# A prefill and decode step of a hybrid attention layer: cached values copied to DRAM before cached keys

## The reference, cut to what matters

```
proj = x @ w_in                                  # (576, 1024) @ (1024, 4096)
q, k, v, g_att, gb, gc, hh, g_conv = split(proj, 8)
o_att = dilated_attention(q, concat(k_past, k), concat(v_past, v))   # windows 128/1, 512/4, 2048/16
att = o_att * silu(g_att)
u = gc * hh;  z = gb * conv3(u) * silu(g_conv)
y = LayerNorm(alpha * x + concat(att, z) @ w_out)
new_k, new_v = the last 2048 rows of concat(k_past, k), concat(v_past, v)
```

## Time and profile before

| | |
|---|---|
| Median of 3 runs | 360.97 us (359.77 to 361.14) |
| The profiled execution | 360.34 us, span 358.5 us |
| Granted clock of TensorE, mean share of full | 0.997 |
| TensorE busy | 348.7 us (97%) |
| VectorE, ScalarE busy | 202.1 us (56%), 117.4 us (33%) |
| DMA moved | 141.06 MB, mean 393 GB/s |
| Of it SyncE's queue q1 | 73.20 MB |
| Of it ScalarE's queue q10 | 67.37 MB |
| Chain that ended last | PE 82%, DMA 6%, DVE 5%, SPq 4%, ACT 1% |

### The profile page before, as it was taken

One profiled execution on the slowest core, in us unless ns is written; L12 is line 12 of the kernel. 1 busy time (PEld: TensorE's weight loads), 2 busy tenths in 40 slices (PEclk: granted clock), 3 DMA queues, 4 the chain that ended last, 5 costly groups with the idle time before them and its releaser, 6 DMA issues.

```text
span 358.5 us, 7719 instructions
## 1 busy us (share of the span) xinstructions
PE 348.7 (97%) x3280; PEld 311.6 (87%) x3280; DVE 202.1 (56%) x381; ACT 117.4 (33%) x233; POOL 11.6 (3%) x28
## 2 busy tenths in 40 slices
PE   8999999999999999999999999999999999899992
PEld 6998888899989888999988889998879988688782
DVE  3724528764145558541446484613546598886774
ACT  4623324352153323421433333214441824330000
POOL 0000000000100000001000000000000004000000
PEclk9999999999999999999999999999999999999998
DMA  8999999999999999999999999999999999999991
GB/s 293 399 429 415 417 415 418 416 423 418 419 421 417 417 413 388 403 420 395 401 416 414 421 419 419 424 423 419 419 414 415 415 402 321 404 345 370 350 324 67
DMA packets 34836, 141.06 MB, mean 393 GB/s; under 512 B 3441, under 2 KB 3825, under 8 KB 32753
## 3 DMA queue, kind: packets, MB, share of 16 engines
q1 hardware_dynamic: 18338, 73.20, 50.8%
q10 hardware_dynamic: 16464, 67.37, 47.6%
HBM read 135.80 MB, written 71.86 MB: 579 GB/s over the span
## 4 chain that ended last, share of the span: by engine, by line
PE 82%; DMA 6%; DVE 5%; SPq 4%; ACT 1%; issue 0%; DVEq 0%; ACTq 0%
PE pj_a L1153 9%; PE pj_b L1153 9%; PE pj_b L1155 8%; PE pj_a L1155 8%; PE pj_a L1154 8%; PE pj_b L1154 8%; DMA wo_raw<-in_w_out 6%; PE sc L1310 4%; PE sc L1346 4%; PE px L1258 3%; PE po L1290 2%; PE pt L1276 2%; SPq L374 2%; SPq L303 2%; PE px L1503 2%; PE px L1504 2%
## 5 line engine op out<-in xcount | busy, mean ns | idle before, releaser
L1153 PE MATMUL pj_b<-x_hi,w_hi 128*128 128x288 f32 x248 | 75.1, 303 | 0.7 <-DVE mix L908 0.7
L1153 PE MATMUL pj_a<-x_hi,w_hi 128*128 128x288 f32 x248 | 75.7, 305 | 0.0
L1154 PE MATMUL pj_a<-x_lo,w_hi 128*128 128x288 f32 x248 | 73.2, 295 | 0.0
L1154 PE MATMUL pj_b<-x_lo,w_hi 128*128 128x288 f32 x248 | 73.1, 295 | 0.0
L1155 PE MATMUL pj_b<-x_hi,w_lo 128*128 128x288 f32 x248 | 73.0, 294 | 0.0
L1155 PE MATMUL pj_a<-x_hi,w_lo 128*128 128x288 f32 x248 | 72.9, 294 | 0.0
L785 DVE TENSOR_TENSOR w_lo<-w_raw,w_hi 128x1024 fp32r<-128x1024 f32 x30 | 36.7, 1223 | 32.3 <-ACT w_hi L472 32.3
L472 ACT CAST w_hi<-w_raw 128x1024 fp32r<-128x1024 f32 x30 | 31.4, 1047 | 69.2 <-DMA w_raw<-in_w_tiles 45.3
L1153 PEld LDWEIGHTS pj_a<-x_hi,w_hi 128*128 128x128 f32 x248 | 46.5, 187 | 6.8 <-issue 6.2
L1153 PEld LDWEIGHTS pj_b<-x_hi,w_hi 128*128 128x128 f32 x248 | 46.5, 187 | 3.1 <-issue 1.1
L1155 PEld LDWEIGHTS pj_b<-x_hi,w_lo 128*128 128x128 f32 x248 | 46.7, 188 | 0.0
(11 more groups left out here) (169 smaller groups left out, 452.5 us busy)
## 6 DMA issues: line engine op xcount, KB each, us to landing
k_buf<-in_k_used SPq DMA_DIRECT2D x16, 1280.0 KB, 15.5
v_buf<-in_v_used SPq DMA_DIRECT2D x40, 512.0 KB, 19.8
out_k_used_out<-in_k_used ACTq DMA_DIRECT2D x16, 1280.0 KB, 18.9
out_v_used_out<-in_v_used ACTq DMA_DIRECT2D x20, 1024.0 KB, 16.6
w_raw<-in_w_tiles SPq DMA_DIRECT2D x30, 512.0 KB, 12.8
out_k_rest_out<-in_k_rest ACTq DMA_DIRECT2D x12, 1024.0 KB, 12.6
out_v_rest_out<-in_v_rest ACTq DMA_DIRECT2D x12, 1024.0 KB, 13.1
wo_raw<-in_w_out SPq DMA_DIRECT2D x8, 512.0 KB, 21.8
```

The costliest lines, as they stand in the source:

```text
L1153: nc.tensor.matmul(out, w_hi[:, w], x_hi[:, c], start=(k == 0), stop=False)
L1154: nc.tensor.matmul(out, w_hi[:, w], x_lo[:, c], start=False, stop=False)
```

## The change

The 24 copies of unused rows stay first. Then come the 20 copies of the sample's values and last the 16 of the keys. The places at which ScalarE issues copies, their number and the final wait are the same.

```
                 n = next(copies)
                 if n < 2 * REST_ROWS:
                     copy_rest(n)
-                elif n < 2 * REST_ROWS + NPAIR * K_PIECES:
+                elif n < 2 * REST_ROWS + NPAIR * V_PIECES // 2:
                     n -= 2 * REST_ROWS
+                    copy_v(n // (V_PIECES // 2), n % (V_PIECES // 2))
+                else:
+                    n -= 2 * REST_ROWS + NPAIR * V_PIECES // 2
                     copy_k(n // K_PIECES, n % K_PIECES)
-                else:
-                    n -= 2 * REST_ROWS + NPAIR * K_PIECES
-                    copy_v(n // (V_PIECES // 2), n % (V_PIECES // 2))
```

## The result

The changed kernel takes 0.6% longer: 362.93 us as the median of 14 runs (361.77 to 365.29), beside 360.72 us for the kernel before on the same chip (14 runs, 359.15 to 362.20). The ratio is 1.0058, 95% interval 1.0040 to 1.0075, which is 1.4 to 2.7 us. The forecast was 364.0 in a range of 361.0 to 367.0. The span of the profiled execution is 361.1 us, 2.6 longer than before.

The account below looks back on a forecast made before the run. TensorE was taken to bound the kernel, with DMA nearly full. Copies 8.0 + 0.6 and stores 1.4 end at 361.2 against 358.15, +3.0 us on 360.34: 363.4, as a median 364.0, range 361.0 to 367.0.

Parts of the forecast that it names:

- The bound and the 2.0 us: TensorE sets the time; its three waits for VectorE, 2.0 us in sum, are the most transfer order can win back.
- rival "faster": Loads of w_out and weights land earlier, TensorE's gaps close, copies end by 355; time 359.0 us, chance 0.05.
- From 144.7 to 302.7: In this stretch the DMA carries less and idles several us; nothing new is asked for, cost to TensorE zero.
- Behind 302.7: In the tail, twelve copies of keys replace smaller ones and lengthen the copies' drain by 8.0 us (7.3 to 8.8).
- high bound: Upper price of the twelve tail copies: time in proportion to bytes at the tail's slow rate, 8.8 us.
- number 47 by itself: Copy 47, issued at 297.3 us, becomes one of keys and lands later by 0.6 us (0 to 2.4).
- The limit of HBM: The skill's limit of about 358 GB/s for one core was not taken as a ceiling for this kernel.
- The last stores: The last tile's two half stores add 1.4 us behind the copies: end at 361.2 against 358.15, +3.0 us.
- The chain under it: Slower stores and ScalarE's full queue delay VectorE's end by 0.5 to 1.5 us, hidden under the copies; nothing added.
- The slack rival: Longer pieces cover pauses between packets, so idle time after the last copy absorbs the cost; 360.3 to 361.5 us, chance 0.28.
- The stuck queue: Slow issues at ScalarE's full queue make VectorE's end slip by over 3 us; time 365 to 368, chance 0.07.
- The signs: Right: DMA share dips, last copy near 360, TensorE's last product about 352. Wrong: product moves over 2 us, VectorE waits long.

Follow-up runs that it names:

- spread: Two of ScalarE's copies moved from ahead of the sample's attention output to behind the second square root; on the changed kernel, 1.0046 of the kernel before.
- spread kernel before: The kernel before, keys still copies 24 to 39, with two of ScalarE's copies moved behind the second square root; 1.0005 of the kernel before.
- late copies cut: The changed kernel with its last twelve copies of keys moving only 1024 of their 1280 KB each; 0.9918 of the kernel before.
- keys at 32: The changed kernel with the copies of keys numbered 32 to 47 in place of 44 to 59; 0.9996 of the kernel before, 0.9935 with spread.
- keys at 36: The changed kernel with the copies of keys numbered 36 to 51 in place of 44 to 59; 0.9993 of the kernel before, 0.9947 with spread.

## Why the prediction was right, point by point

**The bound and the 2.0 us.** TensorE's gaps were read right, but valued wrongly. The prediction had them close only in the rival "faster" (0.05), and expected TensorE's last product at about 352. In fact all three closed, and it starts its last product at 348.8. What was missing is the step that follows from the prediction's own bytes: 4.2 MB less ahead of them let w_out's blocks land after 9.3 us in place of 21.8. Of the 2.9 us between 351.6 and 348.8, the gaps are 2.1 (the products of the second token tile start at 308.57 in place of 310.70). The other 0.7 is a closer spacing of the products behind it, 0.229 us in place of 0.233 from start to start. The spread kernel before has 0.229 too, so this part isn't the order's. The gain can't be seen in the changed kernel's time because the copies end later still. The run with the late copies cut has it (0.9918), as do the keys at 32 and 36, spread.

**From 144.7 to 302.7.** Right in its direction: the rates fall below those of before, by 2.6 MB in sum against 3.15 asked for, and values land sooner. One premise was wrong, that nothing new is asked for in the time won: numbers 48 to 52 left between 297 and 302, where before number 48 left at 302.7, since ScalarE's splits of w_out, which stand ahead of them, came sooner.

**Behind 302.7.** The main term. Forecast 8.0 us between 7.3 and 8.8; measured 43.5 - 35.5 = 8.0 us. The mechanism was right; that the middle of the two bounds was hit to a tenth is luck. The time per MB hardly changed, which speaks for the rule of the high bound (time goes with bytes), and fewer bytes were left than that bound assumed, 2.98 MB more than before in place of 3.15, some of the five early issues having been moved by 302.7. The last copy lands at 360.1, forecast 359.8, so the copies' end moved by 8.9 us and not by 8.0 + 0.6. The 0.9 us beside the 8.0 are the part of the stretch that the copies' queue did not take (13.9 us against 13.0); no row shows the 0.6 us that the forecast had for number 47 by itself.

**The limit of HBM.** The Trainium skill, "DMA: Bandwidth & Descriptors", section "Where 436 GB/s comes from", has about 358 GB/s for one core. With copies alone on the engines 335 to 351 GB/s were seen on one queue and 336 on two; with loads beside them 415 to 419, above that figure. So the figure is near, but as a ceiling on all traffic it does not hold here.

**The last stores.** Mis-sized: 1.4 us behind the last copy were forecast, 0.6 came (360.1 to 360.7). The half store on SyncE's queue finished inside the drain. With the copies' end 0.3 us later this makes 360.7 against 361.2, and +2.6 us in the span in place of +3.0. By the runs it is 2.1 us, interval 1.4 to 2.7.

**The chain under it.** It was put at 0.5 to 1.5 us later for VectorE's end, which came 1.8 us earlier. The delays were real: 5.2 us of waiting for ScalarE's `att_s` in place of 1.2, 1.6 for a square root, 5.3 in place of 4.5 for stores (forecast 1 to 2 us more). Behind TensorE's last product VectorE slipped by 1.0 us, inside the forecast; what was wrong is that TensorE's end would stay. Since neither end decides the time here, this error cost the forecast nothing, and that is luck too.

**The rivals.** The slack rival rested on a pause between packets that longer ones would cover. The changed kernel shows its price directly, in a stretch with copies of keys alone. DMA queues of the changed kernel, 320:325:

```profile
q10 hardware_dynamic: 353, 1.71, 103.0%
```

That is 103.0% of 5 us times 16 by 353, 0.233 us a packet. In the kernel before, in the stretch 315:325 shown above, it is 102.1% of 10 us times 16 by 869, 0.188 us. The rival had forecast 0.186 for keys; the ratio is 1.24, nearly that of the bytes. And two queues of copies, each of which could fill the other's pauses, reached no more than 336 GB/s. The stuck queue is a real mechanism: issues of 8.11 and 6.95 us. It costs little or nothing in the changed kernel (spread, it has 1.0046, its interval overlapping that of 1.0058), and about 0.5% where the copies end earlier (keys at 36: 0.9993 unspread, 0.9947 spread; keys at 32: 0.9996 and 0.9935; all against the kernel before).

**The signs.** Of the signs of being right, the DMA share below 1, the sooner landings ahead of 302.7 and the last copy near 360 came; the chain and TensorE's last product did not. Two signs of being wrong came as well: TensorE's products end more than 2 us away from 352, and a long wait of VectorE for ScalarE stands in the tail. Neither decides the time, since the copies end behind VectorE; they were bad signs to choose, being compatible with the forecast's own mechanism.

What stays open: why the copies alone on the engines run at about four fifths of the mixed rate (335 to 351 GB/s against 415 to 419). No run here varied what they read or write. An estimate from the rows: if a copy's bytes are counted twice, as read from DRAM and as written to it, copies alone make 670 GB/s (2 x 335), and the mixed stretch 190:220 makes some 650 (12.5 MB read and 7.0 MB written in 30 us). A limit on that sum would fit both; it is not shown.

## What to carry to other kernels

When background copies share a full DMA with the loads, their order is a budget over time: bytes pushed to the end cost their full drain once it passes the last compute, and bytes taken from ahead of a critical load pay back. Here the larger ones stood best where the end was not near (keys at 32 and 36), once the places of issue had been moved away from work that others wait for. A gain and a loss of this kind can cancel in the total, so each is best shown by itself before the order is judged.

## What the runs showed of the hardware

Copies from DRAM to DRAM alone on the 16 engines ran at 335 and 351 GB/s from one queue with pieces of 4 KB (kernel before, 315:325 and 335:340), at 343 with pieces of 5 KB (changed kernel, 320:325) and at 336 from two queues (pieces of 5 KB, 330:340). Beside loads into SBUF the sum was 415 to 419 GB/s (kernel before, 105:120 and 190:220).

A DMA issue on ScalarE took 0.58 us, but in the changed kernel up to 8.11 us with six or seven copies under way by their issue and landing times, and what stood behind it on ScalarE waited (7.94 us for a square root). With the same bytes in 320 pieces in place of 256, VectorE waited 7.5 us for `att_s` in place of 5.2 (one profile each).

The Trainium skill, "DMA: Bandwidth & Descriptors", section "Queues, rings and completion order", has the engines go round the queues packet by packet. With two queues of equal pieces the counts were 353 and 350, which agrees. The even counts don't show how many pieces an engine takes from one queue at a time.
